# A fused encoder step on eight cores: the head's order planned with another DMA rate, and stage two's blocks in turns at each weight

## The reference

```
h = RMSNorm_pre(x)
xa, ba, ca, za, xb, zb, ga, gb = split(h @ w_in)             # 8 x 1024 columns
ya = ((ba * conv3(ca * xa)) * silu(za)) @ w_a_out            # short causal convolution
d_g = mean_{W_g}(xb_g) - xb_g ; mixed_g = d_g @ w_grp[g]     # trailing windows 2, 4, 8, 16
yb = (mixed * pool_scale * silu(zb)) @ w_b_out
m = sigmoid(ga) * ya + sigmoid(gb) * yb ; o = m @ w_o
x1 = x + RMSNorm_post(o)
out = x1 + (p @ w_ple) * sigmoid(x1 @ w_pgate)
```

## Time and profile before

| | |
|---|---|
| median of 3 runs | 759.58 us (759.38 to 759.58) |
| the profiled execution | 759.77 us; span of its slowest core (2) 758.2 us |
| spans of the cores | 756.5 to 758.2 us |
| PE (TensorE) busy | 745.3 us, 98% |
| DVE, POOL, ACT busy | 384.3, 339.8, 254.3 us |
| chain that ended last | PE 93%, DMA 4% |

### The profile page before, as it was taken

One profiled execution on the slowest core, in us unless ns is written; L12 is line 12 of the kernel. 1 busy time (PEld: TensorE's weight loads), 2 busy tenths in 40 slices (PEclk: granted clock), 3 DMA queues, 4 the chain that ended last, 5 costly groups with the idle time before them and its releaser, 6 DMA issues.

```text
span 758.2 us, 13217 instructions; the slowest of 8 cores (756.5 to 758.2 us)
## 1 busy us (share of the span) xinstructions
PE 745.3 (98%) x4386; PEld 376.5 (50%) x4386; DVE 384.3 (51%) x639; ACT 254.3 (34%) x514; POOL 339.8 (45%) x514
## 2 busy tenths in 40 slices
PE   6899999999999999999999999999999999999998
PEld 5665454444444444454545545455455555555444
DVE  4775667776622112455557666575751212224655
ACT  3533444442211111333333333343421111115453
POOL 5333555558642433342435536466582342211544
PEclk9999999999999999999999999999999999999999
DMA  8999769858995564827547384474747354306643
GB/s 184 219 149 195 92 156 167 155 109 130 172 156 78 75 92 61 139 76 138 87 85 129 78 135 79 90 132 63 152 84 119 56 80 63 55 0 202 157 119 125
DMA packets 65907, 87.82 MB, mean 116 GB/s; under 512 B 30897, under 2 KB 34737, under 8 KB 65842
## 3 DMA queue, kind: packets, MB, share of 16 engines
q0 software_dynamic: 29792, 50.41, 45.1%
q1 hardware_dynamic: 36050, 36.57, 17.4%
HBM read 117.35 MB, written 11.36 MB: 170 GB/s over the span
## 4 chain that ended last, share of the span: by engine, by line
PE 93%; DMA 4%; POOL 1%; DVE 1%; issue 1%; ACT 0%; SPq 0%; DVEq 0%; ACTq 0%; POOLq 0%
PE ps L604 74%; PE ps L829 8%; PE ps L876 7%; DMA w<-w_in 2%; PE ps L882 2%; DMA wo<-x 2%; PE ps L745 1%; PE ps L575 0%; PE ps L781 0%; POOL sp L713 0%; POOL mT L595 0%; DVE hb L562 0%; DVE sg L894 0%; ACT hb L555 0%; DVE qT L897 0%
## 5 line engine op out<-in xcount | busy, mean ns | idle before, releaser
L604 PE MATMUL ps<-hB,w 128*128 128x512 bf16 (+1 forms) x912 | 156.5, 326 | 0.0
L604 PE MATMUL ps<-hA,w 128*128 128x512 bf16 (+1 forms) x816 | 143.6, 329 | 2.6 <-DVE hA L579 1.9
L604 PEld LDWEIGHTS ps<-hB,w 128*128 128x128 bf16 x912 | 77.1, 98 | 72.0
L604 PE MATMUL ps<-hB,hA 128*128 128x512 bf16 (+1 forms) x624 | 108.6, 326 | 0.0
L604 PEld LDWEIGHTS ps<-hA,w 128*128 128x128 bf16 x816 | 69.2, 98 | 69.0 <-issue 3.7
L808 DVE SCALAR_TENSOR_TENSOR tA<-tA,ps 128x512 f32<-128x512 f32 (+1 forms) x40 | 24.3, 609 | 141.5 <-PE ps L604 141.5
L604 PE MATMUL ps<-hA,mT 128*128 128x512 bf16 x400 | 91.4, 379 | 0.0
L811 POOL TENSOR_TENSOR mT<-tA,tB 128x512 bf16<-128x512 f32 (+1 forms) x40 | 44.0, 1109 | 84.4 <-DVE tB L808 84.0
L604 PEld LDWEIGHTS ps<-hB,hA 128*128 128x128 bf16 x624 | 52.8, 98 | 49.1
L805 ACT ACTIVATE tA<-ps 128x512 f32<-128x512 f32 (+1 forms) x40 | 21.3, 533 | 152.3 <-PE ps L604 147.5
L876 PE MATMUL ps<-wpg,x1T 128*128 128x512 bf16 (+2 forms) x296 | 61.7, 362 | 0.0
(11 more groups left out here) (131 smaller groups left out, 903.0 us busy)
## 6 DMA issues: line engine op xcount, KB each, us to landing
w<-w_in POOLq DMA_DIRECT2D x75, 256.0 KB, 7.3
hA<-w_in POOLq DMA_DIRECT2D x26, 256.0 KB, 8.0
hA<-x SPq DMA_DIRECT2D x10, 512.0 KB, 3.5
y<-hA SPq DMA_DIRECT2D x10, 512.0 KB, 3.8
mT<-w_in POOLq DMA_DIRECT2D x19, 256.0 KB, 8.7
wo<-x SPq DMA_DIRECT2D x9, 512.0 KB, 8.2
wpg<-x SPq DMA_DIRECT2D x8, 512.0 KB, 13.9
w<-w_b_out POOLq DMA_DIRECT2D x14, 256.0 KB, 5.5
```

The source lines that it names most:

```text
L604: ins_ = e.matmul(bk.ap[:, parts[0]:parts[1]], lhsT=w.ap[:, kk, :], rhs=act(kk), start=(kk == 0), stop=(kk == 7))
```

## The change

Four edits, and what they do to the order.

1. `DMA_RATE`, in the planner alone, becomes a step function of the planned time: 0.36, from 4.4 us 0.20, from 7.0 us 0.33, and 0.30 from 46 us on. No instruction has it; it sets the order only.
2. Where groups are cut by tiles, the last two tiles of the second block (6 and 7) become one piece of 256 columns.
3. In stage two the keys of the groups are spread so that all blocks take their turn at a weight before the next weight (not for the last j of the second half).
4. The loads of w_o and w_pgate for j > 1 may not start before the gb group of the first block of the unit before.

The fold's stores to HBM also get a semaphore each.

```
-DMA_RATE = 0.30
+DMA_RATE = ((0.0, 0.36), (4.4, 0.20), (7.0, 0.33), (46.0, 0.30))
+def dma_rate(t):
+    return [r for t0, r in DMA_RATE if t0 <= t + 1e-9][-1]
...
-                for n, tl in enumerate(k.tiles):
+                starts = (0, 1, 2) if k.b else (0, 1, 2, 3)
+                for n in starts:
+                    end = min([c for c in starts if c > n] + [4])
                     for i, g in enumerate(gs):
-                        c0 = n * 128
-                        go = group(key + 1.73 * max(i, n) + 0.1 * n + 0.01 * i, bks[i], 128, (c0, c0 + 128), ws[g],
+                        c0, c1 = n * 128, end * 128
+                        go = group(key + 1.73 * max(i, n) + 0.1 * n + 0.01 * i, bks[i], c1 - c0, (c0, c1), ws[g],
...
+            others = [kb for kb in halves[k.half].blocks if kb is not k] if (k.half, j) != (1, 7) else []
             hv = hT[k.half]
-            g8 = 8 * mm_us(N)
+            g8 = 8 * mm_us(N) + sum(8 * mm_us(kb.N) for kb in others)
+            key = key + sum(8 * mm_us(kb.N) * (1 if others else 4) for kb in halves[k.half].blocks[:k.b])
...
-            ke = key + g8
+            ke = key + 8 * mm_us(N)
...
+        p2_done = []
...
-                   outs=[res(f"{name}{kk}")], dma=0.524, sem=f"ld_{name}{kk}", after=norm_done, tag=f'{name}{kk}')
+                   outs=[res(f"{name}{kk}")], dma=0.524, sem=f"ld_{name}{kk}", after=norm_done + (p2_done[-1:] if j > 1 else []), tag=f'{name}{kk}')
...
-                p2_unit(j, k, wins[(0, 2, j)], kj + k.b * 4 * 8 * MM, all_p1 if j == 0 else ())
+                p2_unit(j, k, wins[(0, 2, j)], kj, all_p1 if j == 0 else ())
+            p2_done.append(H1.blocks[0].p2h[-1])
```

More of the change, by code:

```diff
@@ L222, in ring_step @@
                     return
-                rate = DMA_RATE / len(heads)
-                end = min([dma_t + r[0][1] / rate for r in heads] + nxt + [t])
+                rate = dma_rate(dma_t) / len(heads)
+                end = min([dma_t + r[0][1] / rate for r in heads] + nxt + [t] + [t0 for t0, _ in DMA_RATE if t0 > dma_t + 1e-9])
                 for r in heads:
@@ L238, in ring_next @@
             if heads:
-                rate = DMA_RATE / len(heads)
-                return min([dma_t + r[0][1] / rate for r in heads] + nxt)
+                rate = dma_rate(dma_t) / len(heads)
+                return min([dma_t + r[0][1] / rate for r in heads] + nxt + [t0 for t0, _ in DMA_RATE if t0 > dma_t + 1e-9])
             return min(nxt) if nxt else None
@@ L631, in p1_groups @@
             if tilewise:
-                for n, tl in enumerate(k.tiles):
+                starts = (0, 1, 2) if k.b else (0, 1, 2, 3)
+                for n in starts:
+                    end = min([c for c in starts if c > n] + [4])
                     for i, g in enumerate(gs):
-                        c0 = n * 128
-                        go = group(key + 1.73 * max(i, n) + 0.1 * n + 0.01 * i, bks[i], 128, (c0, c0 + 128), ws[g],
-                                   lambda kk, tl=tl: hv[:, kk, tl.rel:tl.rel + 128], [ws[g], hreg(tl)], n == 0, f'p1t_{j}_{k.b}_{g}_{n}')
+                        c0, c1 = n * 128, end * 128
+                        go = group(key + 1.73 * max(i, n) + 0.1 * n + 0.01 * i, bks[i], c1 - c0, (c0, c1), ws[g],
+                                   lambda kk, c0=c0, c1=c1: hv[:, kk, k.rel + c0:k.rel + c1], [ws[g]] + [hreg(t) for t in k.tiles[n:end]], n == 0, f'p1t_{j}_{k.b}_{g}_{n}')
                         gops.append(go)
@@ L753, in fold @@
                 OP('sp', lambda e, d, w=w, j=j: d(e.dma_start(out=wfold[j * 128:(j + 1) * 128, :].rearrange("p (k c) -> p k c", k=8), in_=w.ap[:])), 0.42, key + 4.0,
-                   ins=[w], outs=[res(f"wfold{j}")], dma=0.26, sem=f"stwf{j % 2}", tag=f'stwf{j}')
+                   ins=[w], outs=[res(f"wfold{j}")], dma=0.26, sem=f"stwf{j}", tag=f'stwf{j}')
                 ws.append(w)
@@ L1050, in build_program @@
             for k in H2.blocks:
-                p2_unit(j, k, wins[(1, 2, j)], kj + k.b * 4 * 8 * MM, ())
+                p2_unit(j, k, wins[(1, 2, j)], kj, ())
             if j == 1:
```

## The result

The changed kernel takes 763.46 us (median of 5, 762.92 to 764.56), the kernel before 759.58 us: a ratio of 1.0051, 95% interval 1.0037 to 1.0064. It is 3.9 us slower, where no change was predicted (759.6 us, range 758.1 to 761.0).

A forecast was written before the change was run, and what follows sets the result against it. TensorE was taken as the bound. Head, merged piece (-0.1) and stage-two wait (-0.74 on core 2) made core 3 slowest at 759.95 us, or core 5 at 759.18; the middle, 759.6 us, was forecast, range 758.1 to 761.0.

The forecast's parts named there:

- The sum: Whole program: core spans 757.65 (core 2), 758.57 (core 3), 757.8 (core 5); slowest plus 1.57 less 0.19 gives 759.95 us.
- the five cases: Tile 4's landing 9 in 100, stage-two wait stays 12, piece priced by weight loads 6, head gains more 13, forecast 60.
- Only three things can move the time: TensorE: when its unbroken run begins in the head, how much work it has, and one 0.74 us wait on core 2.
- One figure of the rivals: Stage two: the change doesn't reach the 0.74 us wait (759.8 us) or moves it to another weight (761.5); 12 in 100.
- The spread (edit 4): Stage two: TensorE's wait for a w_in weight near 214 us goes, 0.74 us on core 2, 0 on cores 3 and 5.
- The head: Start of TensorE's run: tile 3's power op about 0.55 us earlier; net loss 0.29 on core 2, 1.17 core 3, 0 core 5.
- The mechanism that I gave: Head: one 512-column group less ahead of tile 4's transposes, ready 4.80 us after landing; TensorE idles 0.8 us on core 2.
- Fewer fillers: Head: 60 filler matmuls for 68, ahead of tile 1's transposes where TensorE idles 0.97 us; a slower clock ramp costs nothing until then.
- The merged piece: Tiles 6 and 7: eight groups of 128 columns become four of 256, 0.1 us less; bounds 0 and 3.1 us.
- The estimate from the Trainium skill: Merged piece priced from the page's matmul spacings (81 ns for 128 columns, 98 for 256): 2.0 us saved, time 757.7.
- Turns: Stage two: blocks in turns at each weight move groups and add or remove none; worth 0.

## Why the prediction was wrong

**The sum.** The step that failed is the very first: "with 1.57 us around the longest span", and then a sum from TensorE's side alone. It assumed that whatever TensorE does, the span ends the same time after it. A drain of POOL, off that path by 1.5 us, grew by 5.31 us: 5.31 - 1.55 = 3.76 us on core 2, whose span grew by 3.7, and moving two additions off POOL gave 3.1 us of the 3.9 back. The row was in the trace of the kernel before; I did not look behind the last operation. None of the five cases has it. "Only three things can move the time" was false. (One figure of the rivals is added up wrongly: with core 2 at 758.39 core 3, at 758.57, is still the slowest, so the time there is 759.95 us, not 759.8.)

**The spread (edit 4).** I priced it at -0.74 us on core 2. The wait is gone as said; I gave a DMA share of about 0.65 there; it is 0.85 from 230 to 240 us and 0.77 from 200 to 230, still without a new wait. The half more that I added was right, the stretch it was added to was not: from 230 to 260 us the share was 0.53 before, and it is 0.77 now. But I asked of POOL's queue only what stands behind a load in it, not what the queue leaves to be done at the end. And no gain of 0.74 shows in the time with the drain hidden on the slowest core (the kernel before with the spread, POOL ending early): the slowest core of an execution is often one without that wait. (At the place of the order shown above, twelve of the sixteen pieces had been issued before, not ten.)

**The head.** I had a loss of 0.29 to 1.17 us for tile 4's landing on cores 2 and 3, and none on core 5. Tile 3's power came 1.08 us earlier (20.73 for 21.81), not 0.55. The mechanism that I gave did happen, on the cores without the stop. On core 0 tile 4 landed at 25.55, and its transposes waited 0.65 us and began 4.49 us after it, where I had 4.80; on core 1 (24.03) they waited 0.21 us, with the same 4.49; on core 3 (23.48) they were ready just in time. On core 2 it landed at 24.01, 0.8 us earlier than in the execution before, and its transposes waited for nothing: by the same 4.49 us they could have begun at 28.5, and the stop kept TensorE until 29.69. The stop for instructions is the term that I did not have. Five cores have it, 0.2 to 1.3 us, and the kernel before none, though the place is there too. It comes with edit 1: with that undone no core of the execution has it, and the time is about 0.7 us less. How these 0.7 us divide between the stop and the waits for DVE no run tells, nor why the transfer comes later in the new order.

**Fewer fillers.** 0, right: tile 1's transposes began at 16.37 us on core 2, for 16.39.

**The merged piece.** 0.1 us less, right: four groups of 256 and two of 512 take 48.66 - 41.71 = 6.95 us, 4 x 0.87 + 2 x 1.72 = 6.92 by my prices. The estimate from the Trainium skill (TensorE: Matmul & The Clock Gate, section Back-to-back issue gap), 2.0 us less, would have been wrong.

**Turns.** 0, right within the noise: 763.65 us without them (four executions), 763.46 with (five).

**What stays open** is what the queue's part of the drain is. It follows what is issued on POOL's DMA queue, and in what order, and not the number of POOL's instructions or of semaphores; it rises and falls, and it is the same on eight cores. What is worked off there, whether the number of loads or their size counts, and why a burst of sixteen ahead of stage two still shows some 560 us later, no run here tells. That the stop in the head waits for the transfer itself rests on the place being fixed in the stream and on the ends of the transfers, not on a run that took the transfer away.

## What to carry to other kernels

Look behind the last operation: list each engine's drain with its start and length, and know how much slack each has, before a change to a DMA queue is called free. If a drain of POOL is long, let POOL finish early: two additions given to DVE, which had the room, took back 3.1 us. A wait removed on one of eight cores may be worth nothing; see over several executions whether it is on the slowest one.

## What the hardware showed that I had not expected

- POOL's drain at the program's end went on for 3.68, 6.13, 6.78, 8.99, 9.07 or 9.15 us behind POOL's last operation, by what its DMA queue had issued, each within 0.02 us on all cores; in the changed kernel it became shorter by adding loads. The drains of TensorE (1.30 us), DVE (0.31) and ACT (0.29) are nearly all their last operations: at most 0.1 us is behind these. The Trainium skill (VectorE: DVE Perf Modes, section The DRAIN you can't avoid) speaks of drains around a program of about 12 ns on all five engines; SP's 13 ns here is such a value, POOL's is far from it.
- TensorE stopped for 0.2 to 1.8 us at a fixed place in its instruction stream, with no data wait there. 64 waits put ahead moved that place by 64 instructions.
- A wait that is met at once was not free on TensorE: 64 of them, 0.11 us apart, held tile 0's transposes back by 6.7 us on core 1.
